# Four attention stages: both maxima of the next pair of jobs ahead of both scales of the present one

## What is computed

```python
def masked_softmax(s, mask):
    s = jnp.where(mask, s.astype(jnp.float32), NEG_INF)
    m = jnp.max(s, axis=-1, keepdims=True)
    p = jnp.where(mask, jnp.exp(s - m), 0.0)
    return p / jnp.maximum(jnp.sum(p, axis=-1, keepdims=True), TINY)
...
    # MLA (8 heads); NSA selected and window branches (16 heads each)
    s = jnp.einsum('bqhd,bkhd->bhqk', qb, k, preferred_element_type=jnp.float32) * scale
    p = masked_softmax(s, key_pos[None, :] <= q_pos[:, None])
    return jnp.einsum('bhqk,bkhd->bqhd', p.astype(v.dtype), v)
...
    # second block: 4 neighbourhood heads with a bias, 6 dilated heads, 6 grouped-query heads
    mix = jnp.concatenate([rms_norm_2(out_a, ...), rms_norm_2(out_d, ...), rms_norm_2(out_c, ...)], axis=-1)
    return x + mix @ w_out_l
```

## Time and profile before

| | before |
|---|---|
| median of three executions | 1822.44 us |
| the profiled execution's own time | 1822.44 us |
| its span, first to last instruction | 1820.6 us |
| granted TensorE clock, mean over the span | 0.974 |
| PE busy | 1683.6 us (92%) |
| DVE busy | 1022.0 us (56%) |
| ACT busy | 848.5 us (47%) |
| MLA attention | 302 to 320.5 us |
| NSA attention | 825 to 899 us |
| attention of the second block, layer 0 | 1199 to 1246 us |
| attention of the second block, layer 1 | 1547 to 1595 us |

### The profile page before, as it was taken

How to read it: one execution, slowest core, us unless ns; L and a number is a source line. 1 busy time by engine, 2 the same in 40 slices (tenths; PEclk the granted TensorE clock), 3 DMA queues, 4 the chain that set the end, 5 groups by cost and what they waited for, 6 DMA issues and landing times.

```text
span 1820.6 us, 28794 instructions
## 1 busy us (share of the span) xinstructions
PE 1683.6 (92%) x11689; PEld 1525.0 (84%) x11689; DVE 1022.0 (56%) x1303; ACT 848.5 (47%) x1185; POOL 152.3 (8%) x190
## 2 busy tenths in 40 slices
PE   7999997999999999987799998968999997789998
PEld 7999885899989999984589998945999987479997
DVE  6444555444455444767554445665655566665554
ACT  5344465443444333445553444554544454645443
POOL 0000011000000000320000002530000037000000
PEclk9999998999999999998999999989999998999999
DMA  7555441455545555431045555511545564025552
GB/s 265 186 184 184 163 160 47 161 186 184 184 139 209 184 184 171 153 117 47 3 175 187 184 183 145 199 47 47 182 168 201 184 174 156 1 83 196 183 184 93
DMA packets 40546, 276.85 MB, mean 152 GB/s; under 512 B 5505, under 2 KB 6290, under 8 KB 7570
## 3 DMA queue, kind: packets, MB, share of 16 engines
q1 hardware_dynamic: 39010, 271.00, 42.0%
q0 software_dynamic: 1456, 4.72, 1.6%
HBM read 274.65 MB, written 1.05 MB: 151 GB/s over the span
## 4 chain that ended last, share of the span: by engine, by line
PE 82%; DVE 9%; ACT 3%; POOL 3%; issue 1%; DMA 0%; SPq 0%; POOLq 0%; DVEq 0%; ACTq 0%
PE bank L661 19%; PE bank L642 14%; PE bank L643 14%; PE bank L644 14%; PE bank L622 4%; PE bank L573 3%; PE bank L575 3%; PE bank L574 3%; PE bank L718 2%; DVE w_lo L1356 1%; POOL proj L500 1%; PE bank L739 1%; ACT work L1064 1%; PE bank L767 1%; DVE prob L1539 1%
## 5 line engine op out<-in xcount | busy, mean ns | idle before, releaser
L1356 DVE TENSOR_TENSOR w_lo<-raw,w_hi 128x2048 fp32r<-128x2048 f32 x255 | 587.6, 2308 | 531.3 <-ACT w_hi L1054 530.6
L1054 ACT ACTIVATE w_hi<-raw 128x2048 fp32r<-128x2048 f32 x255 | 487.1, 1917 | 549.9 <-PE bank L644 405.1
L642 PE MATMUL bank<-xt_hi,w_hi 128*128 128x256 f32 x2112 | 600.4, 284 | 5.0 <-DVE xt_lo L1388 5.0
L643 PE MATMUL bank<-xt_lo,w_hi 128*128 128x256 f32 x2112 | 598.8, 283 | 0.0
L644 PE MATMUL bank<-xt_hi,w_lo 128*128 128x256 f32 x2112 | 598.6, 283 | 0.0
L642 PEld LDWEIGHTS bank<-xt_hi,w_hi 128*128 128x128 f32 x2112 | 406.2, 192 | 9.1 <-issue 4.9
L643 PEld LDWEIGHTS bank<-xt_lo,w_hi 128*128 128x128 f32 x2112 | 406.4, 192 | 2.5
L644 PEld LDWEIGHTS bank<-xt_hi,w_lo 128*128 128x128 f32 x2112 | 406.4, 192 | 0.0
L661 PE MATMUL bank<-w_hi,h_hi 128*128 128x512 f32 x528 | 208.3, 395 | 0.2
L661 PE MATMUL bank<-w_hi,h_lo 128*128 128x512 f32 x528 | 208.5, 395 | 0.0
L661 PE MATMUL bank<-w_lo,h_hi 128*128 128x512 f32 x528 | 208.2, 394 | 0.0
(11 more groups left out here) (301 smaller groups left out, 1634.5 us busy)
## 6 DMA issues: line engine op xcount, KB each, us to landing
raw<-in_stream SPq DMA_DIRECT2D x255, 1024.0 KB, 4.9
work<-in_rpb POOLq DMA_DIRECT2D x32, 64.0 KB, 3.7
X<-in_x SPq DMA_DIRECT2D x2, 512.0 KB, 4.1
prob<-in_cmp_w POOLq DMA_DIRECT2D x1, 1024.0 KB, 5.2
O<-in_cmp_w POOLq DMA_DIRECT2D x1, 1024.0 KB, 6.9
out<-X SPq DMA_DIRECT2D x1, 1024.0 KB, 4.0
cst<-in_consts SPq DMA_DIRECT2D x1, 776.0 KB, 5.9
O<-in_final_gain POOLq DMA_DIRECT2D x1, 512.0 KB, 3.8
```

The lines of the kernel that those rows point to most:

```text
L642: pe.matmul(o, w_hi[:, sl, cols], xt_hi[:, k, :], start=(k == 0), stop=False)
L643: pe.matmul(o, w_hi[:, sl, cols], xt_lo[:, k, :], start=False, stop=False)
L1054: act.activation(w_hi[:, sl, :], raw[:, sl, :], ACT.Copy).then_inc(hi_done, 1)
L1356: dve.tensor_tensor(w_lo[:, sl, :], raw[:, sl, :], w_hi[:, sl, :].bitcast(F32), ALU.subtract).then_inc(lo_done, 1)
```

## The change

In DVE's loop over the duos, the two maxima of the next duo now stand ahead of the two scales of the present one. Nothing is added or removed, and the other engines' streams are unchanged.

```diff
                 maxima(0)
                 maxima(1)
                 for m in range(n_duos(stage)):
+                    maxima(2 * m + 2)
+                    maxima(2 * m + 3)
                     scale(2 * m)
-                    maxima(2 * m + 2)
                     scale(2 * m + 1)
-                    maxima(2 * m + 3)
                     lo_part(pair_done(stage, m - 2))
                     if stage[:3] == "sec" and m == 6:
                         kind_mean(int(stage[3]), 0)
```

## The result

The changed kernel takes 1903.43 us (median of four, 1902.49 to 1905.59) against 1822.43 us before. The ratio is 1.0446, 95% interval 1.0418 to 1.0474: slower by 81 us, where the prediction had 49. The sign was right, the size was not: 1903 lies outside the range of 1859 to 1889. One of the ten runs of experiment 2 took 2767 us at a granted 0.555 and is outside its ratio.

The account below looks back on a forecast made before the run. The prediction took a ring of PE and DVE waiting for each other once per duo in the attention stages as the bound; 1822.4 + 42.6 (chain) + 6 (clock) = 1871 us, range 1859 to 1889.

Parts of the forecast that it names:

- What bounds the kernel: In the four attention stages, PE and DVE wait for each other once per duo; neither has slack.
- The ring: Scale, transposes, PE's values and scores, next maximum; a steady NSA period takes 4.35 or 3.91 us.
- T0: The moment when DVE starts the maximum of job 2m+2, released by PE's scores.
- cover of scale(2m): Old order does scale(2m) in DVE's idle time before T0, 1.2 us per period; the new order leaves that empty.
- Points 1 to 5, the chain: Longer waits in steady, first, last, dilated and bias duos: MLA 2.6, NSA 18.0, second block twice 11.0, together 42.6 us.
- Point 6, the clock: Longer PE gaps in the second block's dilated periods lower the clock: 6 us taken, from 0 to 14; none in NSA.
- four falls: Clock falls taken among six dilated gaps of the second block, 1.5 us each, 6 us.
- Rival A: The clock falls in NSA too, with 2.0 us of idle per period: 1889 or 1900 us; chance 0.17.
- first version: Rival A with one short fall in each of fifteen NSA periods, 1.2 us each: 18 us, total 1889.
- second version: Rival A with all of NSA at the low clock: 29 us, total 1900; left out of the range.
- B: The clock never falls in the new gaps: 1865 us; low side of the forecast, whose chance including it was 0.76.
- C and D: C: swap hidden in DVE's idle time, 1822 us, chance 0.04. D: ACT sets the ring, faster, 1810 us, chance 0.03.

Follow-up runs that it names:

- experiment 2: Kernel before with useless matmuls on PE, 5 per step in MLA and NSA, 5, 10 and 4 in the second block: 1821.36 us, ratio 0.9982.
- experiment 1: Changed kernel with useless matmuls filling PE's wait ahead of the transposes in all four attention stages: 1861.11 us, ratio 1.0212 to the kernel before.
- `max_pair_middle`: Kernel before with DVE's order scale(2m), maximum(2m+2), maximum(2m+3), scale(2m+1): 1861.05 us, ratio 1.0212.
- `one_max_first`: Kernel before with DVE's order maximum(2m+2), scale(2m), scale(2m+1), maximum(2m+3): 1866.42 us, ratio 1.0244.

## Why the prediction was wrong

*What bounds the kernel* was right. The ring, T0 and the missing cover of scale(2m) are all in the trace after, at +2.76 for +2.79. So are L739's wait for L1536 and the missing wait of ACT for the second maximum.

*Points 1 to 5, the chain*, were right and well sized. With the gaps filled the stages cost 39.9 us more than before. Without the 1.3 us of fillers in the last steps of MLA and NSA that is 37.3, and for the 10 us of low time that before has more, 3.4 us are to be added: 40.7 us, against 42.6 forecast. By stage: MLA 2.7 (forecast 2.6), NSA 17.1 (18.0), the second block 10.3 and 10.7 (11.0 each).

*Point 6, the clock*, is the term that failed, by the low time in it and not by the price of a low us. I took 0.35 us lost per low us from the earlier trace rows; experiment 1 measured 0.34 (0.36 without the fillers of the last steps). I took four falls, about 17 us of low time, and only in the dilated steps. The runs show 114 us of low time more than before, 22 of it in MLA, 54 in NSA and 38 in the second block. The step in the text that did it is "I take no fall there", on the ground that a gap of 2.0 us is reached by no row of either kind; for MLA no fall was even considered. That was reasoning from single gaps, the two of 3.3 us in the earlier trace rows. The gaps came out as long as forecast, 1.9 and 3.5 us, and in NSA the clock was low for about half of most periods, and longer in some.

*Rival A* had the mechanism, and in NSA the amount. Its first version has one short fall of 3.4 low us in each of 15 periods, 18 us; the periods shown have 3.4 to 3.5 low us each, and of NSA's 37.7 us about 20 are not chain. The rest of the way from its 1889 to 1903 lies where A had nothing: some 7 us of clock in MLA, and 14 in the second block where 6 were taken. That its second version, with all of NSA low, said 1900 is luck. The Trainium skill, "TensorE: Matmul & The Clock Gate", section "A second HAM failure mode: psum-queue depth-cycling", says that frequent small idles between groups of matmuls can make the clock swing between its two levels. In NSA of the changed kernel the trace agrees, with a granted 0.74 to 0.76 in the periods shown; the steady NSA of before (waits of 1.06 us) and of `max_pair_middle` (1.59 us), at 1.00, shows that not every such idle does it. I had set A at 0.17 because of the former, which bears on gaps of 1 us and no longer ones. And MLA, with the clock at 0.50 throughout 320 to 330 us, had no fall in any case of the prediction:

```profile
320.00:330.00 10.00, 6.77 (x32) 4.26 (x34) 4.36 (x18) 4.01 (x14) 0.00 (x0) 0.50 0.00 0
```

*B* would have been 1865, which is what the kernel does with its gaps filled (1861). *C and D* were given 0.07 together. Nothing of either showed.

Left open is what makes the clock fall. The length of a gap that comes back doesn't decide it alone: in NSA, waits of 1.06 us (before) and of 1.59 us (`max_pair_middle`) left 1.00, and waits of 1.28 to 1.38 us with a second one of 0.23 us behind them (`one_max_first`) didn't. In MLA it was the other way round: `one_max_first` kept 1.00 with waits of 1.26 us, and `max_pair_middle` fell to 0.50 behind waits of 0.80 and 1.17 us. No run here parts the length of a gap from the work between the gaps.

## What to carry to other kernels

Where two engines wait for each other once per step, find the step's ring and ask of each instruction whether it runs in the ring or in the shadow before it; an order that moves ready work out of that shadow costs its whole length, and one that moves more into it pays at once. Before costing a longer wait on TensorE, count how often it comes back, and price the case in which the clock falls each time: here each us of ring brought about another us of clock. Matmuls of no use in the gap tell the two apart in one run, and here they took the second away.

## What was not expected of the hardware

A wait of 1.9 us that recurs every 7 us kept TensorE at the lower level half of the time in NSA (granted 0.71 over 111 us), while a single one of 3.3 us at 1245.9 left it at 1.00, and so did one of 1.59 us in each of ten periods of `max_pair_middle`. In MLA the clock stayed at 0.50 from 320 to 330 us with PE busy 6.8 of 10 us. With 192 more matmuls in NSA (608 recorded against 416) that stage was 21.5 us shorter than in the changed kernel.
